# The first two weight tiles of each projection, multiplied chunk by chunk in turn

## The reference

```python
h = rmsnorm(x, g) * (1 + sc) + sh      # sc, sh from a vector c through ada_w
y = mixer(h)                           # rwkv7 + pooling (layers 0, 1), gated linear recurrence (2), latent attention (3)
x = x + g1 * y                         # y ends in a projection w_out
h = rmsnorm(x, g) * (1 + sc) + sh
x = x + g2 * peer(h)                   # h @ peer_q, top-16 of 128 x 128 experts in 8 heads, u and v tables of 16384 x 1024
```

## Time and profile before

| | |
|---|---|
| median of 3 runs | 4626.89 us (4625.67 to 4631.51) |
| the profiled execution | 4632.16 us, span 4630.0 us |
| TensorE busy | 4178.7 us, 90% |
| VectorE busy | 3181.3 us, 69% |
| ScalarE busy | 2363.8 us, 51% |
| mean granted TensorE clock | 0.952 of full |

### The profile page before, as it was taken

One profiled execution on the slowest core, in us unless ns is written; L12 is line 12 of the kernel. 1 busy time (PEld: TensorE's weight loads), 2 busy tenths in 40 slices (PEclk: granted clock), 3 DMA queues, 4 the chain that ended last, 5 costly groups with the idle time before them and its releaser, 6 DMA issues.

```text
span 4630.0 us, 84229 instructions
## 1 busy us (share of the span) xinstructions
PE 4178.7 (90%) x30026; PEld 3750.2 (81%) x30026; DVE 3181.3 (69%) x5237; ACT 2363.8 (51%) x3908; POOL 95.5 (2%) x182
## 2 busy tenths in 40 slices
PE   6899996999889999799977999799977799996998
PEld 6889995777889998677767999677764599995777
DVE  6758859776666875977555885877763467858555
ACT  4146648444425665744433665744430156657444
POOL 0000000000000000000000000000000000000000
PEclk8999999999999999999978999999986699999999
DMA  7345550886415554288433555168840045541654
GB/s 265 98 146 177 177 181 10 280 283 216 125 48 158 175 179 141 80 283 281 154 100 113 174 180 180 44 224 282 284 160 9 28 156 176 181 150 37 192 191 151
DMA packets 203621, 748.60 MB, mean 162 GB/s; under 512 B 22704, under 2 KB 23856, under 8 KB 202192
## 3 DMA queue, kind: packets, MB, share of 16 engines
q1 hardware_dynamic: 178416, 646.51, 42.1%
q0 software_dynamic: 25056, 100.15, 7.1%
HBM read 745.52 MB, written 1.05 MB: 161 GB/s over the span
## 4 chain that ended last, share of the span: by engine, by line
PE 81%; DVE 13%; issue 3%; ACT 2%; DMA 1%; DVEq 0%; ACTq 0%; SPq 0%
PE ps L1687 14%; PE ps L1688 13%; PE ps L1689 13%; PE ps L2060 10%; PE ps L2062 10%; PE ps L2061 10%; DVE t_lo L1550 3%; PE ps L1806 2%; DVE oh L1555 2%; DVE arena L1561 2%; DVE t_lo L917 1%; PE ps L1968 1%; PE ps L1970 1%; PE ps L1703 1%; DMA raw<-w_tiles 1%
## 5 line engine op out<-in xcount | busy, mean ns | idle before, releaser
L917 DVE TENSOR_TENSOR t_lo<-raw,t_hi 128x1024 fp32r<-128x1024 f32 x1180 | 1444.7, 1225 | 1097.6 <-ACT t_hi L597 1074.8
L597 ACT CAST t_hi<-raw 128x1024 fp32r<-128x1024 f32 x1180 | 1237.3, 1050 | 1576.4 <-PE ps L1689 808.2
L1687 PE MATMUL ps<-h_hi,t_hi 128*128 128x256 f32 x5344 | 1547.2, 290 | 107.2 <-DVE h_lo L1082 41.3
L1688 PE MATMUL ps<-h_lo,t_hi 128*128 128x256 f32 x5344 | 1525.2, 285 | 0.0
L1689 PE MATMUL ps<-h_hi,t_lo 128*128 128x256 f32 x5344 | 1523.8, 285 | 0.0
L1687 PEld LDWEIGHTS ps<-h_hi,t_hi 128*128 128x128 f32 x5344 | 1036.9, 194 | 132.9 <-issue 108.8
L1688 PEld LDWEIGHTS ps<-h_lo,t_hi 128*128 128x128 f32 x5344 | 1039.6, 195 | 0.7 <-issue 0.5
L1689 PEld LDWEIGHTS ps<-h_hi,t_lo 128*128 128x128 f32 x5344 | 1038.5, 194 | 0.0
L2060 PE MATMUL ps<-t_hi,h_hi 128*128 128x512 f32 x2048 | 815.7, 398 | 16.4 <-DVE t_lo L917 16.2
L2062 PE MATMUL ps<-t_hi,h_lo 128*128 128x512 f32 x2048 | 804.1, 393 | 0.0
L2061 PE MATMUL ps<-t_lo,h_hi 128*128 128x512 f32 x2048 | 803.0, 392 | 0.0
(11 more groups left out here) (280 smaller groups left out, 3029.9 us busy)
## 6 DMA issues: line engine op xcount, KB each, us to landing
raw<-u_tiles SPq DMA_DIRECT2D x512, 512.0 KB, 3.3
raw<-v_tiles SPq DMA_DIRECT2D x512, 512.0 KB, 4.2
raw<-w_tiles SPq DMA_DIRECT2D x188, 512.0 KB, 3.7
oh<-w_tiles POOLq DMA_DIRECT2D x160, 512.0 KB, 4.8
arena<-w_tiles SPq DMA_DIRECT2D x16, 512.0 KB, 4.2
arena<-keys_t POOLq DMA_DIRECT2D x4, 1024.0 KB, 5.0
arena<-mla_w POOLq DMA_DIRECT2D x1, 4096.0 KB, 13.3
arena<-lora POOLq DMA_DIRECT2D x2, 1280.0 KB, 8.1
```

The source lines that it names most:

```text
L597: act.copy(t_hi[:, j % SPL, :], raw[:, j % RAW, :]).then_inc(hi_done, 1)
L917: tts(t_lo[:, j % SPL, :], raw[:, j % RAW, :], t_hi[:, j % SPL, :].bitcast(F32), ALU.subtract).then_inc(lo_done, 1)
L1687: mm(o, hi[:, c, :], h_hi[:, c, :], start=(c == 0), stop=False)
L1688: mm(o, hi[:, c, :], h_lo[:, c, :], start=False, stop=False)
```

## The change

At all thirteen sites the first two tiles are now multiplied together: three matmuls of the first tile for chunk 0, three of the second for chunk 0, then chunk 1, and so on. Before the first matmul TensorE waits until both tiles are lowered and all earlier tiles are read out. `tile_used` is raised once at the last matmul of each of the two, which are now matmuls 45 and 48 of 48.

```diff
-                if fresh and TAKEN[name] == 0:
-                    step(first, first, 0, None, True)
-                    step(first + 1, first + 1, 1, None)
+                def first_two():
+
+                    pe.wait_ge(lo_done, first + 2)
+                    if TAKEN[name]:
+                        pe.wait_ge(taken, TAKEN[name])
+                    for c in range(DC):
+                        seen(h_split)
+                        for n in (first, first + 1):
+                            o = ps[:, n % 2, 0:T]
+                            hi = t_hi[:, n % SPL, :].rearrange("p (c m) -> p c m", c=DC)
+                            lo = t_lo[:, n % SPL, :].rearrange("p (c m) -> p c m", c=DC)
+                            mm(o, hi[:, c, :], h_hi[:, c, :], start=(c == 0), stop=False)
+                            mm(o, hi[:, c, :], h_lo[:, c, :], start=False, stop=False)
+                            ins = mm(o, lo[:, c, :], h_hi[:, c, :], start=False, stop=(c == DC - 1))
+                            if c == DC - 1:
+                                ins.then_inc(tile_used, 1)
+
+                if fresh:
+                    first_two()
                     a = 2
-                elif fresh:
-                    step(first, first, 0, None, True)
-                    a = 1
                 in_loops(pe, name, a, b or count, step)
```

## The result

| | median, us | runs, us | against before |
|---|---|---|---|
| before | 4628.78 | 4, 4625.67 to 4631.51 | |
| after | 4676.31 | 4, 4671.30 to 4677.84 | 1.0101, 95% interval 1.0084 to 1.0119 |

The account below looks back on a forecast made before the run. TensorE, busy 90% of the span and on the chain for 81%, was taken as the bound. 25.9 us late starts + 10.5 clock falls - 2 earlier rise = 34.4 us, giving 4661 us, range 4645 to 4674.

Parts of the forecast that it names:

- the cover: At the thirteen sites, the second tile's matmuls hide the third tile's split; uncovered, it shows 2.46 or 2.85 us.
- The counting by sites: Later start of the third tile, worked out for each of thirteen sites and summed: 25.9 us later.
- an earlier rise of the clock at one or two sites: At one or two of nine norm sites the denser pair brings TensorE's clock up sooner: -2 us.
- The rival that the rise comes at all nine: Clock up nearly from the pair's first matmul at nine norm sites: 19.1 us back, 7 us slower, 4634; chance 0.06.
- filling the feed's gaps gains little: In the first tile, second-tile matmuls fill only TensorE's gaps, 18% idle; at the mixer ends nothing is gained.
- the waits cost nothing: The two added waits before each pair, both tiles lowered and all read out, were met earlier: no cost.
- the delay is carried to the end: After the third tile the delay is neither paid back nor paid again; on one chain, it counts in full.
- I take seven, 10.5 us: Clock falls in the new gap before the third tile at seven of thirteen sites: 10.5 us.
- The price: Cost of one clock fall behind the new gap: 12 matmuls fewer at 0.12 us, 1.5 us.
- The late starts: Third tiles starting later at the thirteen sites: 25.9 us, less 2 us for the clock rising sooner.
- A fall at every site: Rival: the clock falls in the new gap at all thirteen sites, 19.5 us; 45 us slower, 4672; chance 0.10.
- the attention stage: Rival: this 151 us stage, clock 0.51, might run at the upper clock, saving up to 46 us: 4615; chance 0.03.

Follow-up runs that it names:

- the gap filled: Sixteen matmuls the result doesn't need added behind each pair, against the changed kernel: 4656.2 us, ratio 1.0060 to the kernel before.
- the run at the mixer ends alone: The new order only at out0, out1, lout and wo, against the kernel before: 4649.3 us, ratio 1.0043.
- Warming TensorE: Useless matmuls before the first chunk at nine norm sites: added to the kernel before 4631.4 us, to the changed kernel 4665.4 us.
- the parts: The new order at the four mixer ends alone, 4649.3 us, and at the nine norm sites alone, 4659.0 us, each against the kernel before.
- the second profile: The changed kernel run once more without further edit, for another profile: 4677.7 us, ratio 1.0103 to the kernel before.

## Why the prediction was too small

**Right: the cover.** The second tile hid the third's split, and the change takes that away. The counting by sites gave 25.9 us, less 2 for an earlier rise of the clock. The two profiles give 27.8 and 25.7. Timed with the clock's part taken away, it is 27.8 us (the gap filled). Shown.

**Met in number, its cause not shown: an earlier rise of the clock at one or two sites.** In both profiles of the changed kernel in1 has the lower clock for 3.2 to 3.4 us of the pair instead of 6.6, and at no other site is it shorter by as much. But the old order shows it too. This is in1 in the run at the mixer ends alone, which leaves this site as it was:

```profile
1188.94:1197.25 8.31, 8.04 (x48) 7.41 (x49) 7.19 (x21) 4.05 (x9) 0.01 (x1) 0.80 0.85 240
```

The mean of 0.80 over 8.31 us is 3.3 us at the lower clock. So the gain of 2 us may be the scatter between profiles and not the denser pair. The rival that the rise comes at all nine, to which the Trainium skill's rule that activity releases the low clock ("TensorE: Matmul & The Clock Gate", "What's actually happening") would lead in full, didn't occur from the denser pair; only matmuls ahead of h brought the clock up in time, at some of the nine.

**Right: filling the feed's gaps gains little.** At the lower clock the pair is bound by TensorE, and at the mixer ends the feed is fast anyway. At q0 the gap that opened is 2.4 us between starts and the third tile came 1.9 us later, so some 0.5 us were gained. Warming TensorE showed it from the other side: with the clock up the same site came no later than before.

**Right: the waits cost nothing, the delay is carried to the end, the parts add up.**

**The step that failed: "I take seven, 10.5 us", the number of falls behind the new gap.** Seven is the number of the wider gaps (2.5 us idle and more), and those fell at all seven sites in both profiles. The narrower ones (2.1 us idle) were in effect put at nothing, as lying midway between an idle time of 1.58 us that kept the clock and one of 2.81 that lost it; of these six, two fell in the first profile and all six in the second. The price was about right, 1.3 to 1.6 us a fall. The term measured 14.1 and 19.6 us in the two profiles, and some 20 us by the filled gap (47.5 less 27.8), where 10.5 stood.

The late starts were a little short as well: the sum had 23.9 us, the runs 25.7 to 28.3. With 28 instead of 23.9 and 20 instead of 10.5 the sum is 48; since the 20 are the whole less the 28, this is a way to divide the 47.5 us and no second proof. The table of the spans is the independent one. The range ended at 4674 since its upper end joined a fall at every site with the late starts as worked out without the earlier rise, and left 2 us for everything else; the measured 4676.31 lies just beyond. A fall at every site, which had a chance of 0.10, is what the second profile shows.

**Right: the attention stage** kept its clock (0.52 over the same 151 us, 0.51 before), and no rival on the other side came near.

Open is why the same narrow gap loses the clock in one profile and keeps it in the next.

## What to carry to other kernels

Before filling an engine's gaps with the next tile's work, ask what ran under the cover of that work: with two buffers, finishing two tiles together means that the third can't be prepared until both are nearly done. The order pays only where the preparation is shorter than what is left of the second tile, and where the engine is fast enough to be ahead of its feed; here neither held. Mending both, and keeping the new order at six sites only, won back the whole loss and nothing beyond it that could be timed (4.4 us, 0.1%, in the profile). A gap of two microseconds on TensorE had a second price here, in its clock, and filling the gap with useless matmuls was the quick way to measure that price by itself.

## What the runs showed of the hardware

The same kind of gap, between the last matmul of the pair and the first of the third tile, stands in nine profiles of eight kernels, dq and the kernel with the gap filled left out. From start to start it was 2.86 us or more in 30 places, and the lower clock followed in 28 of them (the two others are in1 and lgate with the warming matmuls ahead of the pair); 2.37 to 2.47 us in 21, followed by it in 15, and the same site differed between two profiles of one kernel (q0, q1, q2); 1.29 to 1.88 us in 29, followed by it in none.

A matmul of 128 x 256 in fp32r started every 0.21 us at the lower clock and every 0.12 us at the upper one. Switching the PSUM bank after every three matmuls, with two sums open, cost nothing that the rows show: at out1, all at the upper clock, the last of the 48 matmuls starts 5.70 us after the first, and 5.71 in the old order. Half a cast (512 columns) took 0.62 us against 1.05 for the whole, half a lower 0.69 against 1.23, so by estimate (twice the half less the whole) each instruction carries some 0.15 to 0.2 us of its own.
